# Decoder block on one core: order of the second tokens' index logits around the output transposes, and finer waits in the output projection

## What is computed

```python
# DSA: the indexer picks 64 keys for each token
logits = einsum("bqhd,bkd->bqhk", qi, ki) * 64 ** -0.5
score = einsum("bqh,bqhk->bqk", wi * 8 ** -0.5, relu(logits))
score = where(kpos <= t, score, -inf)
_, sel = top_k(score, 64)
# ... attention over the selected keys gives o_dsa; compressed, selected and window attention give o_nsa
merged = sigmoid(g_nsa) * (o_nsa @ w_br_nsa) + sigmoid(g_dsa) * (o_dsa @ w_br_dsa)
x = x + gate1 * (merged @ w_out)
h = rms_norm(x) * (1 + scale2) + shift2
x = x + gate2 * peer_ffn(h)      # 8 heads, 16 experts each out of 16384, rows of u and v gathered
return rms_norm(x)
```

## Time and profile before

| | us |
|---|---|
| Time, median of 3 executions | 938.74 |
| All three | 938.66, 938.74, 946.12 |
| Profiled execution: span from first to last instruction | 942.2 |
| Profiled execution: its own device time | not given beside the span |
| TensorE busy in the profile | 785.7 (83%) |
| VectorE busy | 654.2 (69%) |
| ScalarE busy | 414.0 (44%) |
| GpSimd busy | 289.5 (31%) |

### The profile page before, as it was taken

One profiled execution on the slowest core, in us unless ns is written; L12 is line 12 of the kernel. 1 busy time (PEld: TensorE's weight loads), 2 busy tenths in 40 slices (PEclk: granted clock), 3 DMA queues, 4 the chain that ended last, 5 costly groups with the idle time before them and its releaser, 6 DMA issues.

```text
span 942.2 us, 9685 instructions
## 1 busy us (share of the span) xinstructions
PE 785.7 (83%) x2880; PEld 424.7 (45%) x2880; DVE 654.2 (69%) x1697; ACT 414.0 (44%) x1157; POOL 289.5 (31%) x262
## 2 busy tenths in 40 slices
PE   2999899999897898888787799888687777877785
PEld 2444678889843453454444355333232222222221
DVE  5532549975688979786767777775967667586756
ACT  3201213350459888542424444555534344343433
POOL 0000000000245443453334354526264342534330
PEclk9899889989999999999999999999799999999998
DMA  9976226772399999999999999999999999999993
GB/s 365 422 313 254 90 89 252 305 318 109 137 423 421 421 421 395 392 419 419 418 419 420 420 419 422 419 422 422 421 423 422 422 421 421 421 421 421 422 422 151
DMA packets 47619, 342.33 MB, mean 363 GB/s; under 512 B 5392, under 2 KB 6608, under 8 KB 11088
## 3 DMA queue, kind: packets, MB, share of 16 engines
q0 software_dynamic: 37152, 268.45, 68.8%
q1 hardware_dynamic: 9968, 72.79, 19.3%
q10 hardware_dynamic: 448, 0.48, 0.2%
HBM read 340.65 MB, written 1.05 MB: 363 GB/s over the span
## 4 chain that ended last, share of the span: by engine, by line
DMA 44%; PE 27%; DVE 16%; ACT 5%; issue 4%; POOL 3%; SPq 1%; POOLq 0%; DVEq 0%
DMA extra<-in_uv,arena 23%; DMA arena<-in_uv,arena 15%; PE banks L788 7%; PE banks L546 5%; PE banks L509 4%; DMA extra<-in_w_ada 3%; DVE extra L1694 3%; DVE arena L1694 2%; POOL extra L907 2%; DMA extra<-in_uv,last_rows 2%; PE banks L728 2%; PE banks L739 2%; PE banks L495 1%; DVE arena L1713 1%; DVE arena L1668 1%
## 5 line engine op out<-in xcount | busy, mean ns | idle before, releaser
L907 POOL DMA_INDIRECT extra<-in_uv,arena x132 | 150.1, 1137 | 436.6 <-DVE arena L1742 249.4
L788 PE MATMUL banks<-extra 128*128 128x512 f32 x472 | 230.7, 617 | 52.2 <-ACT extra L1148 51.2
L788 PE MATMUL banks<-arena,extra 128*128 128x512 f32 x312 | 157.9, 632 | 40.6 <-ACT extra L1148 40.6
L1135 ACT ACTIVATE arena<-arena 128x1 f32<-128x1 f32 x256 | 51.6, 201 | 306.3 <-DVE arena L1694 306.0
L788 PEld LDWEIGHTS banks<-extra 128*128 128x128 f32 x472 | 82.4, 190 | 176.6 <-ACT extra L1148 107.0
L907 POOL DMA_INDIRECT arena<-in_uv,arena x84 | 95.3, 1135 | 137.9 <-PE banks L788 61.0
L1694 DVE CUSTOM_DVE_ANT_0 extra<-extra 128x1024 f32<-128x1024 f32 x75 | 91.4, 1224 | 35.8 <-DMA extra<-in_uv,arena 34.8
L788 PEld LDWEIGHTS banks<-arena,extra 128*128 128x128 f32 x312 | 55.0, 194 | 131.2 <-ACT extra L1148 85.2
L1694 DVE CUSTOM_DVE_ANT_0 extra<-extra,arena 128x1024 f32<-128x1024 f32 x59 | 72.3, 1226 | 43.5 <-DMA extra<-in_uv,arena 43.0
L788 PE MATMUL banks<-ring,extra 128*128 128x512 f32 x152 | 77.9, 642 | 24.2 <-ACT extra L1148 24.2
L1148 ACT ACTIVATE extra<-tab,arena 128x128 f32<-128x128 f32 x234 | 93.9, 401 | 7.7
(11 more groups left out here) (284 smaller groups left out, 1059.1 us busy)
## 6 DMA issues: line engine op xcount, KB each, us to landing
arena<-in_w_late SPq DMA_DIRECT2D x24, 512.0 KB, 8.3
arena<-in_w_ada SPq DMA_DIRECT2D x5, 2048.0 KB, 9.3
arena<-in_w_in SPq DMA_DIRECT2D x4, 2048.0 KB, 21.7
extra<-in_w_gate SPq DMA_DIRECT2D x3, 2048.0 KB, 9.1
extra<-in_w_ada SPq DMA_DIRECT2D x3, 2048.0 KB, 8.5
arena<-in_w_ada SPq DMA_DIRECT2D x4, 1024.0 KB, 11.9
extra<-in_w_ada SPq DMA_DIRECT2D x4, 1024.0 KB, 28.1
extra<-in_w_br SPq DMA_DIRECT2D x2, 2048.0 KB, 14.6
```

The costliest lines, as they stand in the source:

```text
L788: last = nc.tensor.matmul(acc[tt][:, half * 512:(half + 1) * 512], diag[i % DIAGS], uv_slot[SLOT[v]][:, D + half * 512:D + (half + 1) * 51 ...
L907: nc.gpsimd.indirect_dma_start(uv_slot[SLOT[g]], None, A["uv"], bass.IndirectOffsetOnAxis(ap=expert[:, g:g + 1], axis=0)).then_inc(uv_in[S ...
L1135: link(nc.scalar.activation(gel[:, v:v + 1], dots[:, v:v + 1], ACT.Gelu))
```

## The change

`logits(6)` and `logits(7)` move behind `turn_outputs(0)` on TensorE, and their relus behind `turn_copies(0)` on ScalarE. The wait of `mix_out` for all four merges becomes one wait ahead of each pair of k in its first call, in both tiles. On VectorE the six rounds of `select` between the merges stand ahead of merges 1 to 3, where they stood ahead of merges 0 to 2.

```diff
             def mix_out(tt, m):
 
                 w = columns("out", tt, m)
-                pe.wait_ge(merged_ready, 4 * (tt + 1))
                 if m >= 2:
                     pe.wait_ge(x1_ready, KT * tt + m - 1)
                 for k in range(KT):
+                    if m == 0 and k % 2 == 0:
+                        pe.wait_ge(merged_ready, 4 * tt + k // 2 + 1)
                     last = nc.tensor.matmul(B[m % 2][:, 0:P], w[:, k, :], hT[:, k, tt * P:(tt + 1) * P],
                                             start=(k == 0), stop=(k == KT - 1))
                 last.then_inc(mo_done, 1)
@@ TensorE
-            for q in range(4, 8):
+            for q in (4, 5):
                 logits(q)
             turn_outputs(0)
+            for q in (6, 7):
+                logits(q)
             for m in range(KT):
                 branch(0, m)
@@ ScalarE
             open_gates(0)
-            for q in range(4, 8):
+            for q in (4, 5):
                 logit_copy(q)
             turn_copies(0)
+            for q in (6, 7):
+                logit_copy(q)
             open_gates(1)
@@ VectorE
             for q in range(4, 8):
                 score_add(q)
             for i in range(4):
-                if i < 3:
-                    select(1, 2 * i)
-                    select(1, 2 * i + 1)
+                if i:
+                    select(1, 2 * i - 2)
+                    select(1, 2 * i - 1)
                 merge(0, i)
```

## The result

The changed kernel took 936.96 us in the median of 12 executions (933.13 to 942.63), the kernel before 942.29 in 12 (938.66 to 946.12). The ratio is 0.9947 with a 95% interval of 0.9928 to 0.9965: 5.0 us less, between 3.3 and 6.8. The predicted 936.6 us is met to 0.4, but that is partly luck. The three executions shown before the prediction had a median of 938.74, and 12 have 942.29. Two errors cancel here: the base was 3.6 us too low, and the gain, forecast as 2.1 us with bounds of 1.0 and 2.35, is over twice that.

The account below looks back on a forecast made before the run. The gather stream bounds the second part, so an earlier first gather shortens everything. Gains of 0.77 (logits order) and 1.30 (projection waits), 2.1 us together, came off the 938.74 us median: 936.6 us, range 934.8 to 940.5.

Parts of the forecast that it names:

- What bounds the kernel: Whole kernel: the gather stream sets the second part's length; savings ahead move the first gather and everything behind it.
- rival B: Gather stream: the earlier start only meets a hole deeper by 2.1 us, so no change, 938.7 us; chance 0.13.
- The hole at 370 to 390 us: Gather stream at 359 and 364 GB/s instead of 421, worth 2.8 us; expected to move whole with the same depth.
- Part 1: Logits 6 and 7 behind the transposes hide the copy, so branches start 0.77 us earlier; bounds 0.37 to 0.97.
- for it I count nothing, and bound it by 0 and 0.2: Logits 6 and 7: removing their former waits for the relus of 4 and 5 gains 0, at most 0.2 us.
- So yes, by 0.4 us: Output transposes, now 1.97 us earlier: their input `o_ready` is there in time, with 0.4 us margin.
- Part 2: VectorE select rounds one merge later cost nothing, with 0.45 us rest before later merges; cost bounded at 0 to 0.4.
- The cover: VectorE slack: 1.5 us ahead of the first merge despite later score sums, 0.45 us ahead of merges 1 to 3.
- only because the third part of the change takes the two select rounds out: VectorE: with those rounds still in front, the first merge would start at 210.9, 0.5 us late.
- Part 3: Output projection waiting merge by merge fills the 1.38 us gap after the branches: gain 1.30, bounds 1.0 to 1.38.
- the 0.15 to 0.3 us: Output projection: possible lost gain if each added semaphore wait cost 50 to 100 ns in line.
- rival C: TensorE clock returns sooner without pauses before the branches, saving another 1.7 us: 934.9 us; chance 0.08.

Follow-up runs that it names:

- e2: The changed kernel measured once more, no edit; ratio 0.9956 (0.9926 to 0.9986) to the kernel before.
- e4: Changed kernel with only the mix_out wait edit undone, so logits and select rounds moved but one wait for all four merges; ratio 0.9979 to the kernel before.
- e8: Changed kernel with unused matmuls in three TensorE pauses: before the compression matmuls, the first tokens' logits and the queries; ratio 0.9922 to the kernel before.
- e10: Changed kernel with the three pauses of e8 filled and select rounds back ahead of merges 0 to 2; ratio 0.9910 to the kernel before, median 934.16 us.
- e12: The same kernel as e8, measured again for more times and a second profile; ratio 0.9911 to the kernel before.
- e1: The kernel before measured once more, no edit; ratio 1.0022 (0.9999 to 1.0046).
- e3: Kernel before with only the mix_out waits made merge by merge, logits and select rounds in the old order; ratio 0.9992.
- e11: Changed kernel with TensorE waiting for logit 5's relu before the transposes and logit 7's relu before the branches; ratio 1.0003 to the kernel before.
- e6: Kernel before with two unused matmuls in TensorE's pause between output transposes and branches; ratio 0.9987.
- e5: Changed kernel with TensorE waiting for the relu of logit 7 before the first branch; ratio 0.9965 to the kernel before.
- e7: Changed kernel with the select rounds back ahead of merges 0 to 2; ratio 0.9941 to the kernel before.
- e9: Kernel before with unused matmuls in both pauses, two ahead of logit 6 and two ahead of the branches; ratio 0.9999.

## Why the prediction was right and wrong

Stretches of all profiles, in us, read off the timelines (the first column of numbers is a place in the span; the stretch at 0.50 is the one nearest the logits, its start to 0.2 us and its length; the rest is what remains of the span behind the first gather). The upper group has a stretch at 0.50 that began before logits 4 and 5 or while they ran, the middle group one that began after them, the last none:

| profile | first logit record | stretch at 0.50: start, length | logits to first branch | branches | their end to last projection record | from there to first gather | rest |
|---|---|---|---|---|---|---|---|
| before | 200.78 | 199.9, 6.8 | 6.68 | 14.53 | 16.81 | 11.0 | 692.4 |
| e2 after again | 200.49 | 199.6, 6.8 | 5.92 | 14.56 | 15.41 | 12.1 | 692.2 |
| e4 split only | 195.47 | 194.4, 6.8 | 5.89 | 14.56 | 16.81 | 11.0 | 692.9 |
| e8 filled | 195.63 | 194.4, 6.8 | 5.81 | 14.56 | 15.41 | 11.0 | 692.0 |
| e10 filled, select back | 195.29 | 196.0, 3.4 | 4.92 | 14.56 | 15.41 | 11.0 | 691.6 |
| e12 filled | 195.35 | 194.6, 3.4 | 4.41 | 14.56 | 15.41 | 11.0 | 692.0 |
| e1 before again | 198.96 | 200.4, 10.2 | 7.02 | 16.74 | 16.82 | 11.8 | 692.5 |
| e3 waits only | 196.86 | 198.6, 10.2 | 7.02 | 16.94 | 15.41 | 12.1 | 692.1 |
| e11 two pauses | 196.68 | 198.4, 10.2 | 7.45 | 16.76 | 15.40 | 12.0 | 691.4 |
| e6 before, one filled | 196.63 | 198.2, 6.8 | 7.01 | 15.24 | 16.81 | 12.2 | 692.2 |
| e5 one pause | 196.78 | 198.4, 3.4 | 6.18 | 14.56 | 15.40 | 12.0 | 692.5 |
| after | 196.57 | 198.2, 3.4 | 5.40 | 14.56 | 15.41 | 12.0 | 690.9 |
| e7 select back | 194.81 | none | 3.82 | 14.53 | 15.42 | 11.0 | 691.4 |
| e9 before, both filled | 196.87 | none | 6.07 | 14.53 | 16.81 | 11.8 | 691.9 |

**What bounds the kernel.** Right. Behind the first gather the span lasts 690.9 to 692.9 in every profile, wherever the gather stands. A line through the 14 profiles gives it 0.05 us for each us by which the gather comes later, so what the first part saves arrives at the end; rival B fell. The hole at 370 to 390 us did not keep its depth as expected: 388 and 412 GB/s in the changed kernel's profile, where the earlier trace rows have 359 and 364.

**Part 1.** The mechanism was right, the size was not. The step that failed is "for it I count nothing, and bound it by 0 and 0.2", about the waits of logits 6 and 7 for the relus of 4 and 5. It was read from one profile, in which logits 4 and 5 happened to run at half clock, so that ScalarE was nearly ready. At full clock the wait is 1.14. Like compared with like in the table, logits to first branch: where the stretch at 0.50 had begun before logits 4 and 5, the edit takes 6.68 to 5.92 and 5.89 (e2, e4), 0.8 us, as forecast. Where it began after them, it takes 7.02 (e1, e3) to 5.40 (after), 1.6 us. A smaller step failed too: "So yes, by 0.4 us". Where logits 4 and 5 are quick, the transposes come early and wait 0.56 us for `o_ready`.

**Part 2.** The cover was as stated (0.45, and 1.33 for 1.5). But "only because the third part of the change takes the two select rounds out" gave that part a weight that it hasn't: in e7 the first three merges came later, and neither the branches nor the projection waited for them.

**Part 3.** Right: 1.40 us between the traces with and without it, against 1.30. That is the whole gap of 1.38, so the three added waits cost nothing that can be read; the 0.15 to 0.3 us that I drew from the Trainium skill, "Advanced Engine Details and Errata", section "Network/Comms", does not appear.

**The clock.** The sum held the clock fixed, and that was the larger error. I saw the stretch at 0.50 inside the edited one, and gave rival C, that it ends sooner, 0.08. Rival C is what came, beside the larger part 1, and it moves the mean. How much depends on when the stretch begins. Where it had begun before logits 4 and 5, it lasted 6.8 us in both orders (before, e2, e4), and the branches took 14.53 and 14.56. Where it began after them, it lasted 10.2 us and ran into the branches in the three profiles with both pauses (e1, e3, e11: 16.74 to 16.94), 6.8 in e6 with the second pause filled (15.24), and 3.4 in the changed kernel and in e5 (14.56). So the 10.2 us were seen only with both pauses and with a stretch that began after logits 4 and 5. The first profile had one pause, of 0.77, and a stretch that began before them. The Trainium skill, "TensorE: Matmul & The Clock Gate", section "What's actually happening", has activity lift the throttle; e11 agrees, since with the two pauses in it the stretch lasted 10.2 us, where the same order without them had 3.4 and 6.8.

By these profiles the edit is worth 0.8 + 1.4 = 2.2 us in the one kind of execution, which is the forecast, and 1.6 + 2.2 + 1.4 = 5.2 in the other. The gain measured, 5.0 and 4.1 us, lies between, nearer to the second. The times say the same in another way. In the 97 executions of the kernel before that were taken with the experiments the mean was 942.7 us at a mean clock of 0.967, in 24 of the changed kernel 937.9 at 0.972. A line fitted to both with the clock as variable gives 0.52 us for each 0.001 of mean clock, and at equal clock the changed kernel is 2.5 us faster (standard error 0.45). So about half of the gain is schedule, close to the 2.1 forecast, and 0.0045 x 517 = 2.3 us go with the clock. Fitted in the same way, e3 is 1.3 us faster than the kernel before at equal clock and e11 0.6 (standard errors 0.6), near what their schedules alone give: 1.4, and 1.4 less the 0.4 by which its way to the first branch is longer. This split is a correlation; the experiment that shows the cause is e11.

What stays open: how often each length of the slow stretch occurs, since each kernel has one or two profiles; what sets whether it begins before or after logits 4 and 5; and why e9 won no time although its clock rose.

## What to carry to other kernels

A pause of TensorE can cost more than its own length where a stretch of low clock lies beside it: here 128 records behind two such pauses took 2.2 us longer. Price that possibility, and give a reordering that closes pauses there a term for it. Here the gain was about twice what the chain of waits showed. A wait that looks free in one profile may be free only because the work ahead of it was slow in that execution; look at a second profile before bounding it by 0. Where a pause can't be closed, unused matmuls in it can hold the clock. In e8 and e12 they won about 3 us against the changed kernel, in e6 and e9 nothing that the times show.

## What the runs showed of the hardware

- Much of the scatter of this kernel goes with the granted clock. Over the 97 executions of the kernel before the correlation of time and mean clock is -0.77. With three pauses filled ahead of the first gather the standard deviation of the time falls from 2.9 us (before) and 3.2 (changed) to 1.7, 1.1 and 0.3 (e8, e10, e12; 6, 8 and 7 executions).
- TensorE reached the first logit record at 194.8 to 200.8, with no edit ahead of it but fillings, by how long the clock had been low between 108 and 125: none gives 194.8 to 195.6 (e4, e7, e8, e10, e12), 3.4 us 196.6 to 196.9 (six profiles), 10.2 us 198.96 (e1), 13.6 us 200.5 and 200.8 (e2, before).
- Pauses of 0.7 to 1.6 us prolonged a stretch of low clock: 10.2 us with two of them (e1, e3, e11), 6.8 with the second filled (e6), 3.4 without (after), where the stretch began after logits 4 and 5.
- Sparse matmuls alone did not lower the clock: 64 records of 128x30 ran inside a stretch granted 1.00 throughout once the pauses ahead of and behind them were filled (e12), and also in e4 and e7, where they were not.
